# Prompt attention with scores made keys by queries: maxima spread back over the partitions, no transposes of probabilities

## What is computed

```python
def _prompt_attention(q, k, v):          # q, k: (B, T, 8, 96); v: (B, T, 8, 64)
    ...
        s = jnp.einsum('bqhd,bkhd->bhqk', qblk, k).astype(jnp.float32) * ATTN_SCALE
        s = jnp.where(kpos[None, :] <= qpos[:, None], s, -jnp.inf)
        p = jax.nn.softmax(s, axis=-1).astype(v.dtype)
        return jnp.einsum('bhqk,bkhd->bqhd', p, v)
```

## Time and profile before

| | us |
|---|---|
| three runs | 2082.88, 2087.24, 2088.18 (median 2087.24) |
| profiled execution | 2082.69 |
| its span, first to last instruction | 2080.9 |
| TensorE busy in the span | 1993.6 (96%) |
| VectorE, ScalarE, GpSimd busy | 955.6, 767.5, 432.2 |

### The profile page before, as it was taken

The page is one execution under the profiler, slowest core; times in us unless marked ns, Lnnn a source line. Parts: engine busy times, 40 slices in busy tenths (PEclk is TensorE's granted clock), DMA queues, the critical chain, the costliest instruction groups (busy, mean ns, idle before and its releaser), DMA issues. The chain is left out here.

```text
span 2080.9 us, 37740 instructions
## 1 busy us (share of the span) xinstructions
PE 1993.6 (96%) x13328; PEld 1875.8 (90%) x13328; DVE 955.6 (46%) x1703; ACT 767.5 (37%) x1676; POOL 432.2 (21%) x392
## 2 busy tenths in 40 slices
PE   6999997999978999999999699999999999999998
PEld 5999995777758999999999499999999999999998
DVE  6124135565536777777777652323232322223132
ACT  5111234666545666766667332111111111111111
POOL 3232233111010000100000254222222222221221
PEclk7999998999988999999999689999999999999999
DMA  6122000000022222222223111020202111120202
GB/s 216 41 74 62 11 18 10 1 1 0 0 58 70 75 71 74 73 74 74 68 74 125 41 31 41 26 77 16 66 20 60 32 49 50 35 74 7 76 15 98
DMA packets 180601, 108.45 MB, mean 52 GB/s; under 512 B 52132, under 2 KB 177154, under 8 KB 180276
## 3 DMA queue, kind: packets, MB, share of 16 engines
q1 hardware_dynamic: 180358, 107.21, 18.0%
q10 hardware_dynamic: 174, 0.30, 0.1%
HBM read 97.47 MB, written 10.00 MB: 52 GB/s over the span
## 5 line engine op out<-in xcount | busy, mean ns | idle before, releaser
L1750 PE MATMUL banks<-comb_hi,pageT_hi 128*128 128x272 f32 x1024 | 233.8, 310 | 0.0
L1640 DVE TENSOR_REDUCE k_sums<-k_sq 128x8 f32<-128x512 f32 x256 | 174.3, 681 | 91.1 <-ACT k_sq L1462 91.1
L1750 PE MATMUL banks<-comb_hi,pageT_lo 128*128 128x272 f32 x1024 | 212.2, 289 | 0.0
L1750 PE MATMUL banks<-comb_lo,pageT_hi 128*128 128x272 f32 x1024 | 211.8, 288 | 0.0
L2107 DVE TENSOR_TENSOR xT<-xT,banks 128x1074 f32<-128x1074 f32 x64 | 81.5, 1274 | 276.8 <-PE banks L244 276.8
L1462 ACT ACTIVATE k_sq<-banks 128x512 f32<-128x512 f32 x256 | 152.0, 594 | 141.2 <-PE banks L1750 138.2
L1989 ACT ACTIVATE a_hi<-relu 128x1074 fp32r<-128x1074 f32 x32 | 35.4, 1105 | 396.0 <-DVE relu L2095 396.0
L244 PE MATMUL banks<-hf_hi,w_out_up_hi 128*128 128x358 f32 x768 | 169.3, 329 | 0.0
L244 PE MATMUL banks<-a_hi,w_down_lo 128*128 128x358 f32 x768 | 169.1, 328 | 0.0
L244 PE MATMUL banks<-hf_hi,w_out_up_lo 128*128 128x358 f32 x768 | 168.4, 327 | 0.0
L244 PE MATMUL banks<-hf_lo,w_out_up_hi 128*128 128x358 f32 x768 | 168.4, 327 | 0.0
(11 more groups left out here) (368 smaller groups left out, 3936.4 us busy)
## 6 DMA issues: line engine op xcount, KB each, us to landing
page_latents<-in_cache_kv_latent SPq DMA_DIRECT2D x256, 128.0 KB, 2.1
w_out_up_raw<-in_w_up SPq DMA_DIRECT2D x32, 512.0 KB, 4.2
w_down_raw<-in_w_down SPq DMA_DIRECT2D x64, 256.0 KB, 2.7
w_in_raw<-in_w_in SPq DMA_DIRECT2D x17, 512.0 KB, 3.9
x_spill<-xT SPq DMA_DIRECT2D x1, 4296.0 KB, 14.1
xT<-x_spill SPq DMA_DIRECT2D x1, 4296.0 KB, 12.8
page_ropes<-in_cache_k_rope SPq DMA_DIRECT2D x256, 16.0 KB, 1.8
w_out_up_raw<-in_w_o SPq DMA_DIRECT2D x8, 512.0 KB, 4.2
```

The costliest lines, as they stand in the source:

```text
L1640: nc.vector.tensor_reduce(ksum[par][:, j, :], sq[j % 2][:, :].rearrange("p (h c) -> p h c", h=H), AX_X, ALU.add)\
L1750: mm = pe.matmul(banks[:, 2 * (j % 2) + half, 0:WC], x[j % AHEAD][:, k, :], w[par][:, k, half, :], start=k == 0 and a == 0, stop=k == KL - ...
```

## The change

Scores are made with keys on the partitions and queries along the columns, so that the exponentials come out in the form that the value matmul reads; the transposes of probabilities and their copies are gone. Of the score matrix a head computes twelve blocks (`BLOCKS`), which belong to three chunks of queries: 640 to 1039, 256 to 639, 0 to 255. ScalarE copies each block of scores from PSUM to SBUF (`keep_scores`). The maximum over the keys now runs across partitions: VectorE takes the elementwise maximum over all key tiles (`maxima`, into `running_max`), TensorE transposes that, VectorE reduces it (`find_max`), GpSimd writes it onto a diagonal (`diagonal`), TensorE multiplies ones with the diagonal so that every partition holds the maximum of each query (`spread_max`), ScalarE copies it out (`keep_spread`), and GpSimd subtracts it from all scores (`shift`). ScalarE then applies the exponential in place, two blocks at a time. The value matmul has 64 columns of values beside 64 columns of ones, so that the sum of the probabilities comes out on the other 64 partitions. Outputs and sums are copied undivided (`keep_output`), and VectorE divides a pair of heads by its sums (`norm_pair`), during the second head after; the last pair is divided in the next stage, `sample_attention`.

A loop `n` of six steps (`go`) makes the scores of head `n+1`, the units of head `n+2`, the exponentials and values of head `n`; GpSimd prepares queries and keys of head `n+3`. Loops run from -1 to 7; loops 1 to 4 are a hardware loop, the rest are written out. A semaphore's wait on GpSimd, ScalarE or TensorE holds the whole queue of that engine.

```diff
+    top = low.take("running_max", [P, TP], F32)
+    g.sums = low.take("probability_sums", [P, TP], F32)
...
+    CHUNKS = ((640, TP), (256, 640), (0, 256))
+    BLOCKS = [[(k, 640, TP)] for k in range(5)] + [[(k, k * P, TP) for k in (8, 7, 6)], [(5, 640, TP)]] \
+        + [[(k, 256, 640)] for k in range(2)] + [[(k, k * P, 640) for k in (3, 4)], [(2, 256, 640)]] \
+        + [[(k, k * P, 256) for k in range(2)]]
+    CHUNK_OF = [0] * 7 + [1] * 4 + [2]
+    LAST_BLOCK = (6, 10, 11)
+    LAST_GO = (4, 6, 6)
+    NB, GOES, NC = len(BLOCKS), len(BLOCKS) // 2, len(CHUNKS)
...
+    S = [ar.take(f"scoresT{i}", [P, sum(width)], F32) for i in range(2)]
...
+    vh = [ar.take(f"v_and_ones{i}", [P, NT, 2 * VH], F32) for i in range(2)]
+    diag = ar.take("max_diagonal", [P, 400], F32)
+    spread = [ar.take(f"max_spread{i}", [P, 400], F32) for i in range(2)]
...
-    SCORE_BANK = (0, 1, 2, 0, 3, 0, 3, 0, 2)
...
+    def loops(engine, loop):
+        loop(-1, 1, 0, False)
+        loop(0, 0, 0, False)
+        with engine.Fori(0, 2) as i:
+            loop(i * 2 + 1, 1, i, False)
+            loop(i * 2 + 2, 0, i + 1, True)
+        loop(H - 3, 1, (H - 3) // 2, False)
+        loop(H - 2, 0, (H - 2) // 2, True)
+        loop(H - 1, 1, (H - 1) // 2, False)
...
+            def shift(n, par, go):
+                for j in (2 * go, 2 * go + 1):
+                    c = CHUNK_OF[j]
+                    pool.wait_ge(s["max_copied"], n * NC + (c + 1))
+                    for k, q0, q1, at in parts(j):
+                        x = S[par][0:keys_of(k), at:at + q1 - q0]
+                        a = q0 - CHUNKS[c][0]
+                        done = nc.gpsimd.tensor_sub(x, x, spread_of(par, c)[0:keys_of(k), a:a + q1 - q0])
+                done.then_inc(s["shifted"], 1)
...
+            def diagonal(n, c):
+                q0, q1 = CHUNKS[c]
+                tiles, rest = (q1 - q0) // P, (q1 - q0) % P
+                pool.wait_ge(s["max_found"], n * NC + (c + 1))
+                ge(pool, s["max_spread"], n * NC + c)
+                if rest:
+                    nc.gpsimd.tensor_mul(diag[0:rest, tiles * P:tiles * P + rest], ident[0:rest, 0:rest],
+                                         mcol[0:rest, tiles:tiles + 1].broadcast_to([rest, rest]))
+                nc.gpsimd.tensor_mul(diag[:, 0:tiles * P].rearrange("p (a b) -> p a b", b=P),
+                                     ident[:, :].unsqueeze(1).broadcast_to([P, tiles, P]),
+                                     mcol[:, 0:tiles].unsqueeze(2).broadcast_to([P, tiles, P])).then_inc(s["diag_done"], 1)
...
+                for go in range(GOES):
+                    if have(n, 0) and go < GOES - 1:
+                        shift(n, par, go + 1)
+                    if have(n, 0) and go < 2:
+                        diagonal(n, 1 + go)
+                    if have(n, 1) and go == 2:
+                        prepare_v(n + 1, 1 - par)
+                    if have(n, 1) and go == 4:
+                        diagonal(n + 1, 0)
+                    if have(n, 3) and go == 4:
+                        prepare_q(n + 3)
+                    if have(n, 1) and go == 5:
+                        shift(n + 1, 1 - par, 0)
+                    if have(n, 3) and go == 5:
+                        prepare_k(n + 3)
...
+            def keep_scores(n, par, j):
+                act.wait_ge(s["scored"], n * NB + (j + 1))
+                ge(act, s["pv_done"], n * NB - 2 * NB + (j + 1))
+                act.copy(S[par][:, start_of[j]:start_of[j] + width[j]], banks[:, SCORE_BANKS[j % 3], 0:width[j]]).then_inc(s["copied"], 1)
...
+            def probabilities(n, par, go):
+                at, w = start_of[2 * go], width[2 * go] + width[2 * go + 1]
+                act.wait_ge(s["shifted"], n * GOES + (go + 1))
+                act.activation(S[par][:, at:at + w], S[par][:, at:at + w], ACT.Exp, scale=SCALE).then_inc(s["exped"], 1)
...
+                for go in range(GOES):
+                    if have(n, -1) and go == 0:
+                        keep_output(n - 1, 1 - par, before, 1)
+                    if have(n, 1):
+                        keep_scores(n + 1, 1 - par, 2 * go)
+                        keep_scores(n + 1, 1 - par, 2 * go + 1)
+                    if have(n, -1) and go == 0:
+                        keep_output(n - 1, 1 - par, before, 2)
+                    if have(n, 0) and go == 4:
+                        keep_output(n, par, pair, 0)
+                    if have(n, 2) and go < NU:
+                        split_hi(n + 2, par, go)
+                    if have(n, 0) and go in (1, 3):
+                        keep_spread(n, par, 1 if go == 1 else 2)
+                    if have(n, 1) and go == 5:
+                        keep_spread(n + 1, 1 - par, 0)
+                    if go < GOES - 1 and have(n, 0):
+                        probabilities(n, par, go + 1)
+                    if go == GOES - 1 and have(n, 1):
                         probabilities(n + 1, 1 - par, 0)
...
+            def find_max(n, c):
...
+                nc.vector.tensor_reduce(mcol[:, 0:tiles], banks[:, TURN_BANK, 0:tiles * P].rearrange("p (a b) -> p a b", b=P), AX_X,
+                                        ALU.max).then_inc(s["max_found"], 1)
...
+                    nc.vector.tensor_max(top[0:m, q0:q1], top[0:m, q0:q1] if a is None else src[0:m, a:a + w], src[0:m, b:b + w]).then_inc(s["max_steps"], 1)
+                    done += 1
...
+            def norm_pair(pair, go):
+                c, half = go // 2, go % 2
+                q0, q1 = CHUNKS[c]
+                mid = (q0 + q1) // 2
+                if half == 0:
+                    v.wait_ge(s["out_copied"], (pair * 2 + 1) * NC + (c + 1))
+                cols = slice(mid, q1) if half else slice(q0, mid)
+                nc.vector.reciprocal(g.sums[:, cols], g.sums[:, cols]).then_inc(s["sums_inverted"], 1)
+                if half:
+                    v.wait_ge(s["sums_inverted"], pair * (2 * NC) + (go + 1))
+                    x = g.attnT[:, ds(pair, 1), q0:q1].rearrange("p o t -> p (o t)")
+                    nc.vector.tensor_mul(x, x, g.sums[:, q0:q1]).then_inc(s["normed"], 1)
...
+                    if norm:
+                        norm_pair(pair - 1, go)
+                    if have(n, 1):
+                        for j in (2 * go, 2 * go + 1):
+                            done = maxima(n + 1, 1 - par, j, done)
+                    if have(n, 0) and go < 2:
+                        find_max(n, 1 + go)
+                    if have(n, 2) and go < NU:
+                        split_lo(n + 2, par, go)
+                    if have(n, 1) and go == 4:
+                        find_max(n + 1, 0)
...
+            def score(n, par, j):
+                if j == 0:
+                    pe.wait_ge(s["unit_lo_done"], n * NU + NU)
+                ge(pe, s["copied"], n * NB + (j - 2))
+                bank = SCORE_BANKS[j % 3]
+                for k, q0, q1, at in parts(j):
+                    a, m = at - start_of[j], keys_of(k)
+                    keys = slice(k * P, k * P + m)
+                    b = a + q1 - q0
+                    if m < P:
+                        pe.matmul(banks[:, bank, a:b], ident_half[:, :], mask[:, 0:b - a], start=True, stop=True)
+                    for kk, qq, x in ((k_hi, q_hi, 0), (k_hi, q_lo, 1), (k_lo, q_hi, 2)):
+                        if x == 2 and q0 == k * P:
+                            d = min(P, q1 - q0)
+                            pe.matmul(banks[0:m, bank, a:a + d], ident_half[:, 0:m], mask[:, 0:d], start=False, stop=False)
+                        mm = pe.matmul(banks[0:m, bank, a:b], kk[par][0:QK, keys], qq[par][0:QK, q0:q1], start=x == 0, stop=x == 2)
...
+            def spread_max(n, par, c):
+                q0, q1 = CHUNKS[c]
+                pe.wait_ge(s["diag_done"], n * NC + (c + 1))
+                ge(pe, s["max_copied"], n * NC + c)
+                pe.matmul(banks[:, SPREAD_BANK, 0:q1 - q0], g.ones[:, :], diag[:, 0:q1 - q0], start=True, stop=True)\
+                    .then_inc(s["max_spread"], 1)
...
+            def values(n, par, j):
+                c = CHUNK_OF[j]
+                c0 = CHUNKS[c][0]
+                out, first, last = values_bank(par, c), j == 0 or CHUNK_OF[j - 1] != c, j == LAST_BLOCK[c]
+                pe.wait_ge(s["exped"], n * GOES + (j // 2 + 1))
...
+                for go in range(GOES):
+                    if have(n, 1):
+                        score(n + 1, 1 - par, 2 * go)
+                        score(n + 1, 1 - par, 2 * go + 1)
+                    if have(n, 2) and go < NU:
+                        transpose_unit(n + 2, go)
+                    if have(n, 0) and go < 2:
+                        transpose_max(n, 1 + go)
+                    if have(n, 1) and go == 4:
+                        transpose_max(n + 1, 0)
+                    if have(n, 0) and go in (1, 3):
+                        spread_max(n, par, 1 if go == 1 else 2)
+                    if have(n, 1) and go == 5:
```

(27 more changed lines are left out.)

303 lines of the change are left out of this document (137 added, 166 removed).

## The result

| | us |
|---|---|
| before, median of the runs shown with this result | 2085.16 (2082.88 to 2088.18) |
| changed kernel, median of four runs | 2059.26 (2055.05 to 2060.98) |
| ratio of the two | 0.9872, 95% interval 0.9853 to 0.9892 |
| profiled execution, its span | 2060.78, 2059.0 |
| stage, first score matmul to end of the last output copy | 226.8 (before 253.1) |

The change is faster by 25.9 us, and the stage alone is 26.3 shorter; I had forecast 12 for the whole. The time lies inside my range, but the step is over twice what I said. (The spans of the two profiled executions differ by 21.9; of the other 4.4 us, 3.9 lie behind the stage.) The profile after, beginning with the first and the last instruction of the stage and its table of stretches: they answer to the earlier trace rows, with the same columns; the second and third stretch are loops 0 and 1.

A forecast was written before the change was run, and what follows sets the result against it. TensorE, busy 98% of the stage, was taken as the bound, GpSimd as the new main line; start, seven heads and end, 18.5 + 3 x 29 + 2 x 32 + 2 x 28 + 18 = 243.5 against 253.2, gave 2075 us, range 2045 to 2104.

The forecast's parts named there:

- The ring without the lock: Head's chain of engine steps without lock, division or issue gaps: GpSimd's 19.5 us of work plus waits of 0.7 and 4.5.
- The price of the subtractions: GpSimd subtracting the maximum from 4,752 columns: 2.17 ns a column plus 0.19 us, 12.6 us per head.
- the second wait: GpSimd, after its last subtraction, waits for the next head's first maximum, late in VectorE's queue: 4.5 us per head.
- the first: GpSimd waits ahead of a diagonal for VectorE's reduction of head n's second chunk: 1.1 us, counted as 0.7.
- The three issue gaps per head: TensorE's delay in starting after a wait, three times on each head's path, 0.17 us each.
- The lock and the division: VectorE's maxima take 3.7 us of GpSimd's time per head; reciprocals ahead of maxima add 3 us in heads 2 and 4.
- 0 for the reciprocals: VectorE's in-place SBUF reciprocals cost GpSimd nothing through the lock; upper bound 7.4 us for each of three pairs, 22 us.
- GpSimd, the new main line: After the change GpSimd's queue sets the head: 19.5 us of subtractions, diagonals and preparation, plus lock and waits.
- One of my signs of being wrong: ScalarE waiting for exponentials would make GpSimd's price per column the failed term.
- (a): Rival: lock and waits cheaper, about 24 us per head, 5 less in seven heads, 2040 us; 20%.
- (b): Rival: TensorE's gaps drop its clock, 1.7 us per fall; one per head gives 2087, two 2099; 27%.
- (c): Rival: GpSimd's queue and VectorE's reciprocals make 30.5 to 31.5 us per head, no gain, 2081 to 2090; 13%.

The follow-up runs named there:

- e1: Changed kernel with the elementwise maxima taking their new operand from the PSUM bank of the scores, not the SBUF copy; 2036.63 us, ratio 0.9771.
- e5: e3 plus a GpSimd wait, ahead of preparing values in step 2, for VectorE's maximum of block 4 of the next head; 2049.56 us, ratio 0.9833.
- e7: e1 without the division of head pairs 0 to 2; 2034.33 us, ratio 0.9761.
- e3: Changed kernel without the division (reciprocals and multiplications on VectorE) of head pairs 0 to 2; 2068.49 us, ratio 0.9930.
- e8: e1 without GpSimd's preparation of keys and values for heads 2 to 7; 2036.23 us, ratio 0.9768.
- e6: e1 with the next head's first maximum moved forward: transposes and reduction to step 4's start, spreading matmul and copy ahead of step 5's scores; 2019.28 us, ratio 0.9691.
- e11: e6 with ScalarE copying the second chunk's output ahead of the next head's first exponential, no longer behind it; 2014.35 us, ratio 0.9666.
- e2: Changed kernel with only the transposes and reduction for the next head's first maximum moved to the start of step 4; 2058.82 us, ratio 0.9876.
- e4: Changed kernel without GpSimd's preparation of keys and values for heads 2 to 7; 2050.99 us, ratio 0.9846.
- e9: Maximum moved forward as in e6, but maxima read both operands from SBUF as in the changed kernel; 2054.60 us, ratio 0.9862.

## Why the prediction was right or wrong

**The kind of change and what moved** were right: TensorE off the bound, the longest wait ahead of the next head's first diagonal, and the last pair's normalisation hidden in the next stage (behind its multiplication VectorE still idles 1.80 us for TensorE). The heads are 25.1 to 31.0 us apart, where I had 28 to 32.

**The sum was 16.7 us too long** (243.5 against 226.8). Cut as I cut it, by GpSimd's first subtraction of head 0 (361.60) and of head 7 (553.03): start 16.8 us (I had 18.5), seven heads 191.4 (207), end 18.5 (18). The heads are the miss.

**The ring without the lock came out near.** My terms without it are 18.5 + 5 x 24.7 + 2 x 23.8 + 18 = 207.6; e1 measures 205.3, of which the seven heads take 170.2 (171.1 in my terms). The price of the subtractions fits (I had 1.05 us for 400 columns, e1 1.04), the second wait is a little shorter (4.5; in e1 2.9 to 4.2 in loops 0 to 5), the first a little longer (0.7 a head; in e1 7.1 us in all). The three issue gaps per head, 3.5 us in all, have no room in that comparison.

**The lock and the division were mis-sized**, and this is the step that failed: 7 x 3.7 + 2 x 3 = 31.9 us in my sum, and 226.8 - 205.3 = 21.5 measured. That is 10.4 of the 16.7 us; the issue gaps are 3.5 more. Of the 21.5 some 3 us at most are the clock's: it fell in five places of the changed kernel's stage and in two of e1's, at about 1 us each (e5). The mean of 3.1 per head is near my 3.7, but the mechanism as I put it is wrong. I had each maximum let in after one GpSimd operation and GpSimd paying for it. In the runs GpSimd pays about a sixth, VectorE waits for one operation, for two or for six, and the price of a head lies between 1.0 and 6.5 us (the loops of the changed kernel less those of e1: 1.7, 6.5, 3.0, 2.7, 4.6, 1.0, 2.1). The division's 3 us in loops 2 and 4 are next to nothing without the lock (loops 2 and 4 are 0.2 us shorter in e7), and with the lock leaving them out costs 8.5 (e3). My "0 for the reciprocals" against GpSimd was right: 0.93 us for 128 columns beside it and alone. What was wrong is the 3 us for their place in VectorE's queue. The Trainium skill (SBUF — State Buffer, Who interferes with whom) says that a VectorE instruction with at most one SBUF input, outside the two-port modes, does not contend with GpSimd, and that one with two SBUF inputs contends with a GpSimd instruction that reads SBUF. The trace agrees with the first by the reciprocals' 0.93 us, with the second by the 1013 and 563 ns of the maxima.

**"GpSimd, the new main line" was wrong in substance, though its arithmetic gave the right period.** 19.5 of work and 5.2 of waits make 24.7, but 3.0 less work leaves 24.6 (e8). One of my signs of being wrong did come: ScalarE waits for subtractions ahead of its exponentials, 32.4 us in all in the changed kernel's stage. I had put it down to a wrong price per column, but that price fits, and 22.0 us of these waits remain in e1; so the sign doesn't single out the price. The period is set by the ring: subtraction, exponential, output and score copies in ScalarE's order, maximum, spread, subtraction. e6 and e11 show two of its links, the way of the maximum and ScalarE's order, by shortening them; the others I read from the waits. A sum of one engine's work and its waits says how long a head is, not what would shorten it.

**The rivals.** (a) Lock and waits cheaper, 2040: of the three it came nearest to what happened, a smaller lock with the waits as they were, but its 24 us a head is reached only without the lock. (b) The clock: it fell five times in the stage, in loops 1, 3, 4, 6 and the end, for 3.4 us each. Ahead of these falls TensorE had stood idle for 3.71 us (loop 1), 1.76 to 1.94 (loops 3, 4, 6) and 3.02 (the end); other gaps of 1.74 to 1.98 brought none. The stretch of loop 1's gap, and the one after it (clock in the third column from the right):

```profile
402.50:406.20 3.70, 0.03 (x1) 0.00 (x0) 3.60 (x6) 0.59 (x2) 1.64 (x3) 1.00 0.01 2
406.70:410.10 3.40, 3.40 (x9) 2.10 (x7) 0.69 (x1) 1.70 (x3) 1.15 (x2) 0.50 0.00 0
```

So my sign for (b), a clock of 0.5 inside the stage, came, but not its price: a fall costs about 1 us (e5) and not 1.7, and my point of decision was a second fall in a head; there was at most one. In e6 and e11, with no gap over 1.5 us, it did not fall at all once the first scores were made. (c) did not come.

**What stays open**: what decides whether VectorE is let in after one instruction, after two or after six. The eleven maxima of over 5 us in the changed kernel, e2, e3, e4 and e9 are all those of block 4, beside the same six instructions, and all began 0.1 to 0.2 us ahead of GpSimd's next instruction (398.92 against 399.02); but others that began so were let in sooner (1.35 and 1.75 us in loop 5 and later). Another kind waits through the large diagonal and the queries' preparation, two instructions, as this one of the changed kernel, beside GpSimd from 470.24 to 472.67:

```profile
470.21 2.88 DVE L1263 TENSOR_TENSOR running_max<-running_max,scoresT 128x384 f32<-128x384 f32 x1 [0.22 <-ACT scoresT L1148]
```

No run tests it.

## What to carry to other kernels

Where VectorE and GpSimd work beside each other, count VectorE's operands in SBUF: taking one from PSUM, where the data stood anyway, was worth 21.5 us of a stage of 227, more than any one reordering. Before you move steps forward, take such a coupling out: with it the same reordering gave 0.4 us of stage (4.7 by the medians, not clear of the noise), without it 18. And test a "main engine" by taking work from it: if its waits grow by as much, the bound lies elsewhere, here in a ring over several engines, and the order on these is where time lies.

## What the runs showed of the hardware

- An operation of VectorE with two operands in SBUF can be held for six GpSimd instructions in a row, 5.66 us for one of 0.5, until GpSimd's queue ran dry. In e3 it recurred in five heads running, always with the same maximum.
- The lock is not symmetrical: over the stage the maxima lost 52 us, the subtractions 10 (changed kernel less e1).
- Less work can take longer: e3 leaves out some 32 us of VectorE's work (22 of reciprocals, 10 of multiplications) and is 9 us slower than the changed kernel in the median; a wait added to it (e5) makes it 19 us faster.
- A fall of TensorE's clock to 0.5 for 3.4 us made a loop of 26 us 1.0 us longer in e5, and no longer in e4.
